# The mixer's latents, recurrence queries and first output turned by VectorE and a round trip through DRAM

## Chip, cores and metric

The kernel runs on one core of one Trainium2 chip. The metric is the device time of one execution in microseconds. The kernel before takes 1125.22 us, the median of three runs (1125.12 to 1125.36).

## What is computed

One layer of a streaming encoder on 256 tokens of width 2048, all float32. Cut to what matters here:

```python
h = rms_norm(x, attn_norm_w)
hq, hf, hi, hg, c_q, c_kv, k_r = split(h @ w_in)          # 1024 x4, 512, 512, 64
# first mixer: gated linear recurrence, 8 heads of 128
q = silu(hq); f = lb + (1 - lb) * sigmoid(hf); k = 1 - f
S_t = diag(f_t) S_{t-1} + k_t i_t^T;  o_t = S_t^T q_t
o_a = rms_norm(o, norm_w) * silu(hg)
# second mixer: latent attention, 8 heads
q = rms_norm(c_q, q_norm_w) @ w_uq;  kv = rms_norm(c_kv, kv_norm_w) @ w_ukv
o_b = softmax(masked(rope(norm(q)) @ rope(norm(k)).T)) @ v
x = x + concat([o_a, o_b]) @ w_out
x = x + (silu(n @ w_gate) * (n @ w_up)) @ w_down,  n = rms_norm(x, ffn_norm_w)
```

## The kernel before

Tokens lie on the partitions in two tiles of 128 (NT = 2). TensorE contracts over partitions, so every left operand has to be turned: features on the partitions, tokens in the row. Float32 precision comes from a split: a number is a rounded part "hi" and a rest "lo", and a product is hi x hi, lo x hi and hi x lo.

The weights come through a ring of four slots (`raw`, loaded by SyncE's queue, 512 KB each). ScalarE casts a slot to `w_hi` (line 757 up to the first eleventh of the feed-forward, 977 after), VectorE subtracts to `w_lo` (lines 1084, 1532). One slot is a granule: TensorE multiplies it in 12 matmuls (lines 1693, 1696). Granules 0 to 136 are the projections `lat` (3 blocks: the two latents and the rotary key), then hq0, uq0, hf0, ukv0, hi0, uq1, hg0, ukv1, hq1, uq2, ukv2, hf1, uq3, ukv3, hi1, hg1, then `w_out`. ScalarE may cast granule n only when TensorE is done with n - 4, and both conversions are written three granules ahead of TensorE (LEAD = 3).

Everything else in the mixers is a list of small steps, `schedule()`, each with a position, which is a granule's number. Each of the three engines goes through the same list in the same order: at position g, ScalarE and VectorE first convert granule g + 3 and then do their part of the steps of g, and TensorE does its part and then multiplies granule g. Within an engine all is in order, so a step that waits holds up the conversions behind it. END[block] is the number of the first granule behind a block: 17 and 25 for the blocks that complete the first and the second latent, 33 for hq0, 43 for hf0, 73 for hq1, 85 for hf1.

The steps that matter:

- `lat_a`, `lat_b` (18, 19 for the first latent, 26, 27 for the second): squares on ScalarE, reciprocal root, and the latent scaled by VectorE (line 1205). `lat_t` (22 and 30, two steps each): TensorE turns the latent in eight transposes through its identity matmul (line 1716) into PSUM banks, ScalarE writes the big half `mT_hi` (line 804), VectorE the small half `mT_lo` (line 1105). uq0 needs the first at granule 33, ukv0 the second at 43.
- `angles`, `sines` (29, 30): rotary angles, a long chain on VectorE, then ScalarE. `lb_a` to `lb_c`: the gates' lower bounds. `kr_b` (34): the rotary key.
- `hq` (33 and 73): the recurrence queries by ScalarE (line 897). `turn` (45 and 46 for the first half g = 0, 89 and 91 for the second): TensorE transposes queries (n = 0) and gates (n = 1) (line 1794), ScalarE copies them (line 905) or makes keys and logs (907, 910).
- `q_a`, `q_b`, `q_t` (35, 36, 39 for the first pair of heads): norm and rotation of attention queries into `stage` on VectorE, which TensorE transposes at position 39 (line 1751).
- `scan`, `lev_a`, `lev_b`, `pairs` (from 48 and 95): decays of the recurrence on VectorE and ScalarE, their products on TensorE (line 1805 for level 1).
- `o_a`, `o_b` (80, 81 for g = 0): norm of the recurrence's output, written to E by line 1403. `scores`, `softmax` (83, 84 for head 4), `hf_a` (84 for g = 1): forget gates, ScalarE 897, VectorE 1300 and 1301. `o_t` (95 for g = 0): eight transposes of the output and its split.

Small results of TensorE go through four side banks in turn; `side_uses` says which steps take one and who gives it back. The feed-forward already turns its hidden values as the change does: VectorE turns 32x32 blocks (line 1475), POOL writes them to DRAM and reads them back in four parts (lines 712, 718), with the same sizes.

Of the kernel before, what the change touches and what calls it, by code (L numbers as in the profile page):

```python
# [24 lines left out]
F32 = mybir.dt.float32  # L25
# [6 lines left out]
P = 128  # L32
D = 2048
SEQ = 256
NT = SEQ // P
# [179 lines left out]
def schedule():  # L215
# [32 lines left out]
    for g in range(2):  # L248
# [3 lines left out]
        s += [(e + 2 + 2 * g + n * (1 + g), ("turn", g, n, t)) for n in range(2) for t in range(NT)]  # L252
# [10 lines left out]
        s += [(p, ("o_a", g)), (p + 1, ("o_b", g))]  # L263
# [63 lines left out]
SPLIT = {step: n for n, step in enumerate(SPLITS)}  # L327

# [31 lines left out]
def hybrid_layer(nc, x, positions, attn_norm_w, w_in, hgrn_lb, hgrn_norm_w, mla_q_norm_w, w_uq, mla_kv_norm_w,  # L360
# [7 lines left out]
    with ExitStack() as ctx:  # L368
        def sb(name, shape, dt=F32, where=ctx):
            return where.enter_context(nc.sbuf_tensor(name, shape, dt))  # L370
# [75 lines left out]
        latents = (lat, hv)  # L446
        qTn = X[:, 0, :].rearrange("p (h t) -> p h t", h=HEADS)
# [9 lines left out]
        squares = nc.dram_tensor("squares", (P // Q, Q, P // Q, SEQ), F32, kind="Internal").ap()  # L457
        first_two = sb("first_two", [P, WIDE])
# [7 lines left out]
        corner, partly, both = gate[:, 0, :], gate[:, 1, :], hidden[:, 0, :]  # L466

# [45 lines left out]

        s_turned = sem("s_turned")
# [132 lines left out]
        def _(pool):  # L647
# [50 lines left out]

            pool.wait_ge(s_x[len(PIECES) - 1], 16)
            pool.dma_start(lb[:, :, :], hgrn_lb[:, 0:GW].partition_broadcast(P)).then_inc(s_lbin, 16)  # L700

            pool.wait_ge(s_lbused, 1)
            pool.wait_ge(s_side, USE[("join8", 0)] + 1)
            pool.dma_start(lb[:, :, :], hgrn_lb[:, GW:2 * GW].partition_broadcast(P)).then_inc(s_lbin, 16)

            pool.wait_ge(s_side, USE[("scores", HEADS - 1)] + 1)
# [41 lines left out]
        def _(act):  # L748
# [48 lines left out]

            def split_hi(parts):
# [8 lines left out]
            def step(s):  # L807
# [30 lines left out]
                elif kind == "lat_t":  # L838
                    i, j = a
                    ps, k, col = filled(s), 4 * i + 2 * j, (V_KVN if i else V_QN) + 2 * j  # L840
                    split_hi([(mT_hi[:, k + n, :], ps[:, n * SEQ:(n + 1) * SEQ], col + n) for n in range(2)])
# [46 lines left out]
                elif kind in ("hq", "hf_a", "hi", "hg"):  # L888
# [3 lines left out]
                    if kind == "hq" and not a[0]:  # L892
                        act.wait_ge(s_side, USE[("lat_t", 0, 1)] + 1)
                    if a[0] and kind == "hg":
                        act.wait_ge(s_given["dve"], GIVEN[USE[("o_a", 0, NT - 1)]])
# [3 lines left out]
                elif kind == "turn":  # L899
# [3 lines left out]
                    src = filled(s)[:, :].rearrange("p (h t) -> p h t", h=GH)  # L903
# [41 lines left out]
                elif kind == "o_t":  # L945
                    g, j = a
                    dst, k = (hT_hi, 12 + 2 * j) if g else (mT_hi, MT[HEADS + 2 * j])
                    split_hi([(dst[:, k:k + 2, :], filled(s)[:, :].rearrange("p (k t) -> p k t", k=2), V_HG)])
# [122 lines left out]
        def _(dve):  # L1071
# [26 lines left out]
            def split_lo(s, parts):  # L1098
# [8 lines left out]
                ins.then_inc(s_tlo, 1)  # L1107

                dve.wait_ge(s_tlo, SPLIT[s] + 1)
                dve.sem_inc(s_given["dve"], 1)  # L1110
# [61 lines left out]
            def step(s):  # L1172
# [33 lines left out]
                elif kind == "lat_t":  # L1206
                    i, j = a
                    ps, k, col = filled(s), 4 * i + 2 * j, (V_KVN if i else V_QN) + 2 * j
                    split_lo(s, [(mT_lo[:, k + n, :], ps[:, n * SEQ:(n + 1) * SEQ], mT_hi[:, k + n, :], col + n)
                                 for n in range(2)])  # L1210
# [98 lines left out]
                elif kind == "lev_a":  # L1309
# [3 lines left out]
                    if l == 1:  # L1313
                        if g:
                            dve.wait_ge(s_side, USE[("o_t", g - 1, 1)] + 1)
# [91 lines left out]
                elif kind == "o_t":  # L1407
                    g, j = a
                    hi, lo, k = (hT_hi, hT_lo, 12 + 2 * j) if g else (mT_hi, mT_lo, MT[HEADS + 2 * j])
# [623 lines left out]
```

## Time and profile before

| | us |
|---|---|
| median of three runs | 1125.22 |
| profiled execution | 1124.67 |
| span of the profiled execution, first to last instruction | 1122.9 |
| TensorE busy | 1113.2 |
| VectorE busy | 886.8 |
| ScalarE busy | 640.5 |
| granted TensorE clock | 1.0 |

Times of rows are counted from the span's start. The steps above end near 468 us; the feed-forward takes the rest. In a row of a timeline the first number is the start, the second how long the row lasts (several instructions when it ends in x2 or more), and a bracket at its end gives the engine's idle time before it and what ended that. PE is TensorE's matmuls, PEld its weight loads, DVE is VectorE, ACT ScalarE, POOL GpSimd.

### The profile page before, as it was taken

How to read it: one execution, taken by the hardware profiler on the slowest of the kernel's cores; microseconds unless marked ns; L12 is line 12 of the kernel's file. 1: busy time of each engine (PE TensorE's matmuls, PEld its weight loads, DVE VectorE, ACT ScalarE, POOL GpSimd, SP SyncE). 2: the span in 40 equal slices, each digit the busy share in tenths (PEclk: the TensorE clock that was granted, in tenths of full speed). 3: DMA queues.
4: the chain of work that ended last, by engine and by line, in shares of the span. 5: the costliest groups of instructions: out<-in, count | busy, mean ns of one | idle time of the engine just before them, and what ended most of it. 6: DMA issues, size and time to landing. Idle time of an engine off the chain costs nothing.

```text
span 1122.9 us, 15465 instructions
## 1 busy us (share of the span) xinstructions
PE 1113.2 (99%) x5265; PEld 937.8 (84%) x5265; DVE 886.8 (79%) x1198; ACT 640.5 (57%) x907; POOL 51.1 (5%) x134
## 2 busy tenths in 40 slices
PE   7999999999999999999999999999999999999998
PEld 7988888888888888888888888888888888888887
DVE  5578786587876667688888888888988879889777
ACT  7566776668664556454554554554554555555553
POOL 3000000000000000000000000000000010000000
PEclk9999999999999999999999999999999999999999
DMA  8666455545555455667777677777777686666655
GB/s 267 192 196 189 158 159 156 164 141 170 197 177 168 153 187 169 212 212 234 225 229 237 222 232 238 222 229 236 224 235 226 224 276 217 207 206 199 211 190 169
DMA packets 107239, 228.99 MB, mean 204 GB/s; under 512 B 8201, under 2 KB 19250, under 8 KB 106930
## 3 DMA queue, kind: packets, MB, share of 16 engines
q1 hardware_dynamic: 101346, 209.30, 58.9%
q0 software_dynamic: 5536, 18.88, 5.8%
q8 instruction: 29, 0.48, 0.2%
q14 instruction: 24, 0.20, 0.0%
q10 hardware_dynamic: 304, 0.14, 0.0%
HBM read 218.32 MB, written 9.96 MB: 203 GB/s over the span
## 4 chain that ended last, share of the span: by engine, by line
PE 97%; DVE 2%; DMA 1%; ACT 0%; issue 0%; SPq 0%; DVEq 0%; ACTq 0%
PE side L1919 25%; PE main L1693 22%; PE side L1921 12%; PE main L1696 11%; PE side L1891 4%; PE side L1892 4%; PE side L1893 4%; PE main L1893 3%; PE main L1891 3%; PE main L1892 3%; PE side L1817 1%; PE side L1716 1%; DMA raw<-in_w_in 1%; PE side L1764 0%; PE side L1765 0%; DVE w_lo L1084 0%
## 5 line engine op out<-in xcount | busy, mean ns | idle before, releaser
L977 ACT CAST w_hi<-raw 128x1024 fp32r<-128x1024 f32 (+1 forms) x245 | 241.6, 990 | 172.2 <-PE side L1919 104.9
L1532 DVE TENSOR_TENSOR w_lo<-raw,w_hi 128x1024 fp32r<-128x1024 f32 (+1 forms) x245 | 275.4, 1139 | 21.9 <-ACT w_hi L977 21.6
L1084 DVE TENSOR_TENSOR w_lo<-raw,w_hi 128x1024 fp32r<-128x1024 f32 (+3 forms) x156 | 178.5, 1154 | 107.9 <-ACT w_hi L757 105.6
L757 ACT CAST w_hi<-raw 128x1024 fp32r<-128x1024 f32 (+3 forms) x156 | 153.7, 993 | 142.5 <-PE main L1693 137.6
L1693 PE MATMUL main<-w_hi,hT_hi 128*128 128x512 f32 (+2 forms) x448 | 173.4, 388 | 1.7 <-DVE hT_lo L1105 1.4
L1696 PE MATMUL main<-w_hi,hT_lo 128*128 128x512 f32 (+2 forms) x448 | 169.1, 378 | 0.0
L1921 PE MATMUL side<-w_hi,hT_lo 128*128 128x512 f32 x400 | 155.6, 389 | 0.0
L1919 PE MATMUL side<-w_hi,hT_hi 128*128 128x512 f32 x400 | 155.6, 389 | 0.0
L1693 PE MATMUL main<-w_lo,hT_hi 128*128 128x512 f32 (+2 forms) x448 | 114.6, 377 | 0.0
L1919 PE MATMUL side<-w_lo,hT_hi 128*128 128x512 f32 x400 | 106.9, 389 | 0.0
L1693 PEld LDWEIGHTS main<-w_hi,hT_hi 128*128 128x128 f32 x448 | 84.7, 189 | 15.5 <-DVE hT_lo L1105 1.8
L1696 PEld LDWEIGHTS main<-w_hi,hT_lo 128*128 128x128 f32 x448 | 84.8, 189 | 13.0
L1693 PEld LDWEIGHTS main<-w_lo,hT_hi 128*128 128x128 f32 x448 | 82.9, 189 | 14.1
L1919 PEld LDWEIGHTS side<-w_hi,hT_hi 128*128 128x128 f32 x400 | 75.1, 188 | 15.6
L1919 PEld LDWEIGHTS side<-w_lo,hT_hi 128*128 128x128 f32 x400 | 75.1, 188 | 15.6
L1921 PEld LDWEIGHTS side<-w_hi,hT_lo 128*128 128x128 f32 x400 | 75.1, 188 | 15.5
L1921 PE MATMUL side<-w_hi,aT_lo 128*128 128x512 f32 x208 | 80.9, 389 | 0.0
L1919 PE MATMUL side<-w_hi,aT_hi 128*128 128x512 f32 x208 | 80.9, 389 | 0.0
L1532 DVE TENSOR_TENSOR w_lo<-last_two,w_hi 128x1024 fp32r<-128x1024 f32 x36 | 44.1, 1225 | 43.5 <-ACT w_hi L977 43.5
L977 ACT CAST w_hi<-last_two 128x1024 fp32r<-128x1024 f32 x36 | 37.9, 1052 | 59.9 <-PE side L1919 59.9
L977 ACT CAST w_hi<-first_two 128x1024 fp32r<-128x1024 f32 x36 | 38.0, 1056 | 58.4 <-PE side L1919 58.4
L1693 PE MATMUL main<-w_hi,mT_hi 128*128 128x512 f32 (+1 forms) x160 | 62.0, 387 | 0.0
(279 smaller groups left out, 1819.0 us busy)
## 6 DMA issues: line engine op xcount, KB each, us to landing
raw<-in_w_gate_up SPq DMA_DIRECT2D x176, 512.0 KB, 4.8
raw<-in_w_down SPq DMA_DIRECT2D x88, 512.0 KB, 4.5
raw<-in_w_in SPq DMA_DIRECT2D x64, 512.0 KB, 3.8
raw<-in_w_out SPq DMA_DIRECT2D x32, 512.0 KB, 3.7
raw<-in_w_in SPq DMA_DIRECT2D x15, 384.0 KB, 4.5
squares<-hiddenT POOLq DMA_DIRECT2D x11, 512.0 KB, 5.0
hiddenT<-squares POOLq DMA_DIRECT2D x44, 128.0 KB, 5.3
raw<-in_w_ukv SPq DMA_DIRECT2D x8, 512.0 KB, 3.9
```

The source lines that it names most:

```text
L757: copy(w_hi[:, slot, 0:n], raw[:, slot, 0:n]).then_inc(s_hi, 1)
L977: copy(w_hi[:, n % RING, 0:cols], src).then_inc(s_hi, 1)
L1084: tt(w_lo[:, slot, 0:n], raw[:, slot, 0:n], w_hi[:, slot, 0:n].bitcast(F32), ALU.subtract)\
L1532: tt(w_lo[:, n % RING, 0:cols], src, w_hi[:, n % RING, 0:cols].bitcast(F32), ALU.subtract)\
L1693: m = matmul(banks[t][:, 0:cols], hi[:, at[n], tok], rhs, start=(part == "hi" and k == k_first), stop=(part == "lo" and k == last))
L1696: matmul(banks[t][:, 0:cols], lo[:, at[n], tok], rhs, start=False, stop=False)
L1716: m = transpose(ps[:, at:at + P], where[:, t, (k + n) * P:(k + n + 1) * P], ident[:, :])
L1891: matmul(bank, hi, big, start=first, stop=False)
L1892: matmul(bank, lo, big, start=False, stop=False)
L1893: return matmul(bank, hi, small, start=False, stop=last)
L1919: m = matmul(bank, hi, rhs, start=False, stop=(part == "lo" and (t, half) in last))
L1921: matmul(bank, lo, rhs, start=False, stop=False)
```

## The change

Forty transposes leave TensorE: `lat_t` of both latents, `turn` with n = 0 of both halves, `o_t` of g = 0. In their place stands a new step, `swap`: VectorE turns the 128x1024 values in 32x32 blocks, POOL writes the result to DRAM (512 KB) and, once that has landed, reads it back in four parts of 128 KB that put the blocks where they belong. Positions: `swap` of the latents at 19 and 27, of the queries at 34 and 84, of the output at 81. The consumers wait for the landing: `lat_t` moves to 26, 27 (first latent) and 34, 35 (second), `turn` with n = 0 is at 45 and moves from 89 to 90 for g = 1, `o_t` stays at 95. The latents' and the output's small halves are made in four instructions of 128x128 a step. The turned data borrow buffers that are free at the time (`hbT`, `hkT`, E, `hgate`), which brings a few waits of order. POOL does the five round trips in the order first latent, second latent, queries 0, then the second load of the gate bounds, output 0, queries 1. All else is as before.

```diff
@@ schedule()
-        s += [(e + 1, ("lat_a", i)), (e + 2, ("lat_b", i))] + [(e + 5, ("lat_t", i, n)) for n in range(2)]
+        s += [(e + 1, ("lat_a", i)), (e + 2, ("lat_b", i)), (e + 2, ("swap", "lat", i))]
+        s += [(e + 9 + n, ("lat_t", i, n)) for n in range(2)]
...
-        s += [(e + 2 + 2 * g + n * (1 + g), ("turn", g, n, t)) for n in range(2) for t in range(NT)]
+        s += [(e - g if g else END[("hq", g)] + 1, ("swap", "hq", g))]
+        s += [(e + 2 + 3 * g + n, ("turn", g, n, t)) for n in range(2) for t in range(NT)]
...
-        s += [(p, ("o_a", g)), (p + 1, ("o_b", g))]
+        s += [(p, ("o_a", g)), (p + 1, ("o_b", g))] + [(p + 1, ("swap", "o", g))] * (g == 0)
@@ side_uses(step)
-    if kind in ("x", "x2", "lat_t", "o_t"):
+    if kind in ("x", "x2") or kind == "o_t" and step[1]:
         return [(step, "dve")]
-    if kind in ("vec", "turn", "probs_t", "join7", "join8"):
+    if kind in ("vec", "probs_t", "join7", "join8") or kind == "turn" and step[2]:
         return [(step, "act")]
@@ POOL
+            def swap(*key):
+
+                n, at = SWAP[key], swap_of[key]
+                pool.wait_ge(s_swap, n + 1)
+                pool.dma_start(swapped[n].rearrange("a c b x -> (a c) b x"), at).then_inc(s_parked, 16)
+                pool.wait_ge(s_parked, 16 * (n + 1))
+                for b in range(P // Q):
+                    pool.dma_start(at[Q * b:Q * (b + 1), :, :], swapped[n, :, :, b, :].rearrange("a c x -> c a x"))\
+                        .then_inc(s_landed, 16)
@@ ScalarE
+            def landed(*key):
+                act.wait_ge(s_landed, MOVED * (SWAP[key] + 1))
...
-                    ps, k, col = filled(s), 4 * i + 2 * j, (V_KVN if i else V_QN) + 2 * j
-                    split_hi([(mT_hi[:, k + n, :], ps[:, n * SEQ:(n + 1) * SEQ], col + n) for n in range(2)])
+                    k, col = 4 * i + 2 * j, (V_KVN if i else V_QN) + 2 * j
+                    landed("lat", i)
+                    split_hi([(by_quarter(mT_hi[:, k + n, :]), swapped_tile(("lat", i), 2 * j + n), col + n)
+                              for n in range(2)])
...
                     if n == 0:
-                        copy(hqT[:, :, t * P:(t + 1) * P], src).then_inc(s_given["act"], 1)
+                        landed("hq", g)
+                        src = swap_of[("hq", g)].rearrange("p a (t h r) -> p t h a r", t=NT, r=Q)[:, t, :, :, :]
+                        copy(hqT[:, :, t * P:(t + 1) * P].rearrange("p h (a r) -> p h a r", r=Q), src)
@@ VectorE
+            def swap(key, src):
+
+                nc.vector.transpose(swap_of[key].rearrange("p b (n r) -> p n b r", r=Q),
+                                    src.rearrange("p t (k b c) -> p (t k) b c", b=P // Q, c=Q)).then_inc(s_swap, 1)
...
-                    split_lo(s, [(mT_lo[:, k + n, :], ps[:, n * SEQ:(n + 1) * SEQ], mT_hi[:, k + n, :], col + n)
-                                 for n in range(2)])
+                    k, col = 4 * i + 2 * j, (V_KVN if i else V_QN) + 2 * j
+                    split_lo(s, [(by_quarter(mT_lo[:, k + n, :])[:, t, :, :], swapped_tile(("lat", i), 2 * j + n)[:, t, :, :],
+                                  by_quarter(mT_hi[:, k + n, :])[:, t, :, :], col + n) for n in range(2) for t in range(NT)])
@@ TensorE
-                elif kind == "lat_t":
-                    i, j = a
-                    pe.wait_ge(s_lat, NT * (i + 1))
-                    turn_x(s, 2 * j, latents[i])
...
-                elif kind == "turn":
+                elif kind == "turn" and a[1]:
...
-                elif kind == "o_t":
+                elif kind == "o_t" and a[0]:
```

## Rows read from the trace of the kernel before

**Rows 1.** The page, engines: busy us, share of the span, instructions.
```profile
PE 1113.2 (99%) x5265; PEld 937.8 (84%) x5265; DVE 886.8 (79%) x1198; ACT 640.5 (57%) x907; POOL 51.1 (5%) x134
```

**Rows 2.** The page, chain that ended last, by engine.
```profile
PE 97%; DVE 2%; DMA 1%; ACT 0%; issue 0%; SPq 0%; DVEq 0%; ACTq 0%
```

**Rows 3.** The page, groups: busy us, mean ns, idle before and its releaser.
```profile
L1084 DVE TENSOR_TENSOR w_lo<-raw,w_hi 128x1024 fp32r<-128x1024 f32 (+3 forms) x156 | 178.5, 1154 | 107.9 <-ACT w_hi L757 105.6
```

**Rows 4.** Transposes of queries (16) and first latent (8): ns min/median/max, first and last start.
```profile
L1794 PE MATMUL side<-ident,lat x16: 270/273/275, 116.5 to 265.5; 128*128 128x128 f32 x16
L1716 PE MATMUL side<-ident,lat x8: 270/272/273, 55.5 to 56.2; 128*128 128x128 f32 x8
```

**Rows 5.** Timeline of the weight loads around the first latent's transposes.
```profile
55.34 0.94 PEld L1716 LDWEIGHTS side<-ident,lat 128*128 128x128 f32 x8
...
56.24 0.19 PEld L1693 LDWEIGHTS main<-w_hi,hT_hi 128*128 128x128 f32 x1
```

**Rows 6.** Instructions on the feed-forward's turned values, waits, and time to landing.
```profile
L1475 DVE STREAM_TRANSPOSE hiddenT<-hidden x11: 1233/1235/1240, 471.3 to 895.1; 128x1024 f32<-128x1024 f32 x11
...
DMA squares<-hiddenT: 53.4, 11
...
DMA to landing us min/median/max: 3.4/5.3/7.2
```

**Rows 7.** Timeline of POOL, first round trip of the feed-forward.
```profile
472.86 0.57 POOL L712 DMA_DIRECT2D squares<-hiddenT  x1 [173.26 <-DVE hiddenT L1475]
478.57 2.20 POOL L718 DMA_DIRECT2D hiddenT<-squares  x4 [5.14 <-DMA squares<-hiddenT]
```

**Rows 8.** Timelines of ScalarE and VectorE: both halves now, four 128x128 elsewhere.
```profile
56.69 1.56 ACT L804 ACTIVATE mT_hi<-side,vec_cols 128x256 fp32r<-128x256 f32 x4
...
57.96 0.87 DVE L1105 SCALAR_TENSOR_TENSOR mT_lo<-side,vec_cols,mT_hi 128x256 fp32r<-128x256 f32 x2
...
123.34 1.13 DVE L1263 SCALAR_TENSOR_TENSOR stage<-main,stat,kw_row 128x128 f32<-128x128 f32 x4
```

**Rows 9.** Timeline of VectorE, 50 to 100 us.
```profile
52.94 0.89 DVE L1205 TENSOR_SCALAR lat<-lat,stat 128x512 f32<-128x512 f32 x2
...
73.87 1.23 DVE L1084 TENSOR_TENSOR w_lo<-raw,w_hi 128x1024 fp32r<-128x1024 f32 x1 [1.34 <-ACT w_hi L757]
...
90.62 1.23 DVE L1084 TENSOR_TENSOR w_lo<-raw,w_hi 128x1024 fp32r<-128x1024 f32 x1 [2.78 <-ACT w_hi L757]
...
98.65 0.28 DVE L1140 TENSOR_TENSOR stage_r<-rot 128x128 f32<-128x128 f32 x1
```

**Rows 10.** Timeline of ScalarE, 60 to 90 us.
```profile
64.64 1.05 ACT L757 CAST w_hi<-raw 128x1024 fp32r<-128x1024 f32 x1 [1.69 <-PE main L1693]
65.59 0.63 ACT L779 ACTIVATE hlf<-hv 128x512 f32<-128x512 f32 x1
...
84.59 1.06 ACT L757 CAST w_hi<-raw 128x1024 fp32r<-128x1024 f32 x1 [1.35 <-PE main L1693]
```

**Rows 11.** Timeline of TensorE: the query stage's first transposes.
```profile
99.45 0.60 PE L1751 MATMUL side<-ident,stage 128*128 128x128 f32 x4
```

**Rows 12.** Timeline of ScalarE, last wait for TensorE before the recurrence's first half.
```profile
111.27 1.05 ACT L757 CAST w_hi<-raw 128x1024 fp32r<-128x1024 f32 x1 [1.67 <-PE main L1693]
```

**Rows 13.** Line 1805, level 1 products: what TensorE waited for (us, times).
```profile
DVE E L1339: 0.5, 1
```

**Rows 14.** Timeline of VectorE, 245 to 262 us.
```profile
245.72 2.16 DVE L1403 SCALAR_TENSOR_TENSOR E<-side,stat,hgate 128x128 f32<-128x128 f32 x8
...
257.43 1.23 DVE L1300 TENSOR_TENSOR hlf<-hlf,E 128x1024 f32<-128x1024 f32 x1 [1.83 <-ACT hlf L897]
...
259.84 2.35 DVE L1084 TENSOR_TENSOR w_lo<-raw,w_hi 128x1024 fp32r<-128x1024 f32 x2
```

**Rows 15.** Timeline of TensorE, granule whose w_lo starts at 259.84.
```profile
261.20 0.47 PE L1693 MATMUL main<-w_hi,mT_hi 128*128 128x512 f32 x1
```

**Rows 16.** The page: busy tenths of the DMA engines in 40 slices of 28 us.
```profile
DMA  8666455545555455667777677777777686666655
```

More of the change, by code:

```diff
@@ L327 @@
 SPLIT = {step: n for n, step in enumerate(SPLITS)}
+SWAPS = [step[1:] for _, step in SCHEDULE if step[0] == "swap"]
+SWAP = {key: n for n, key in enumerate(SWAPS)}
 RMS = [step for _, step in SCHEDULE if step[0] in ("r1a", "lat_a", "q_a", "k_a", "o_a", "r2a")]
@@ L446, in hybrid_layer @@
         latents = (lat, hv)
+        swap_of = {("lat", 0): hbT[:, :, :], ("lat", 1): hkT[:, :, :], ("o", 0): hgate.rearrange("p t (a c) -> p (t a) c", a=2)}
+        for g in range(2):
+            swap_of[("hq", g)] = E[:, g, :].rearrange("p (a c) -> p a c", a=P // Q)
         qTn = X[:, 0, :].rearrange("p (h t) -> p h t", h=HEADS)
@@ L512, in hybrid_layer @@
         s_join = sem("s_join")
+        s_swap = sem("s_swap")
+        s_parked = sem("s_parked")
+        s_landed = sem("s_landed")
         s_turned = sem("s_turned")
@@ L891, in step @@
                                "hg": (hgate, ACT.Silu)}[kind]
-                    if kind == "hq" and not a[0]:
-                        act.wait_ge(s_side, USE[("lat_t", 0, 1)] + 1)
+                    if kind == "hq":
+                        act.wait_ge(s_swap, SWAP[("hq", 0) if a[0] else ("lat", 0)] + 1)
                     if a[0] and kind == "hg":
-                        act.wait_ge(s_given["dve"], GIVEN[USE[("o_a", 0, NT - 1)]])
+                        act.wait_ge(s_tlo, SPLIT[("o_t", 0, 1)] + 1)
                     for t in range(NT):
@@ L946, in step @@
                     g, j = a
-                    dst, k = (hT_hi, 12 + 2 * j) if g else (mT_hi, MT[HEADS + 2 * j])
-                    split_hi([(dst[:, k:k + 2, :], filled(s)[:, :].rearrange("p (k t) -> p k t", k=2), V_HG)])
+                    if not g:
+                        landed("o", g)
+                        split_hi([(by_quarter(mT_hi[:, MT[HEADS + 2 * j + n], :]), swapped_tile(("o", g), 2 * j + n), V_HG)
+                                  for n in range(2)])
+                        return
+                    k = 12 + 2 * j
+                    split_hi([(hT_hi[:, k:k + 2, :], filled(s)[:, :].rearrange("p (k t) -> p k t", k=2), V_HG)])
                 elif kind == "sq2":
@@ L1408, in step @@
                     g, j = a
-                    hi, lo, k = (hT_hi, hT_lo, 12 + 2 * j) if g else (mT_hi, mT_lo, MT[HEADS + 2 * j])
-                    split_lo(s, [(lo[:, k:k + 2, :], filled(s)[:, :].rearrange("p (k t) -> p k t", k=2),
-                                  hi[:, k:k + 2, :], V_HG)])
+                    if not g:
+                        at = [MT[HEADS + 2 * j + n] for n in range(2)]
+                        split_lo(s, [(by_quarter(mT_lo[:, k, :])[:, t, :, :], swapped_tile(("o", g), 2 * j + n)[:, t, :, :],
+                                      by_quarter(mT_hi[:, k, :])[:, t, :, :], V_HG)
+                                     for n, k in enumerate(at) for t in range(NT)])
+                        return
+                    k = 12 + 2 * j
+                    split_lo(s, [(hT_lo[:, k:k + 2, :], filled(s)[:, :].rearrange("p (k t) -> p k t", k=2),
+                                  hT_hi[:, k:k + 2, :], V_HG)])
                 elif kind in ("out1", "out2"):
```

44 lines of the change are left out of this document (33 added, 11 removed).

## The prediction

> **What bounds the kernel now.** The page comes first: TensorE is busy for 99% of the span, VectorE for 79% [rows 1], and the chain that ended last is TensorE for 97% [rows 2]. So time taken off TensorE comes off the kernel, as long as nothing else makes TensorE wait. Next, what TensorE depends on. Each step of the first 137 ("granules", 12 matmuls each) needs its weights split by ScalarE (w_hi) and then VectorE (w_lo). The groups by line show that VectorE spends 107.9 us waiting ahead of w_lo, nearly always for w_hi [rows 3]: on average there is room. But both queues run in order, with the mixer's small steps between the conversions, so the average says little; the timelines of ScalarE and VectorE have to be followed where the edited steps stand. There the reader should look at the bracket at the end of a row: it is the idle time ahead of the instruction. A stretch without brackets has no room, and whatever is put into it arrives later at the far end. "ACT waits for PE main" is the good case: the engine has caught up and is paced by TensorE.
>
> **What is removed.** 40 transposes on TensorE: 8 for each of the two latents, 16 for the recurrence queries [rows 4], 8 for the first output, all of one form. Eight of them hold the weight-load queue from 55.34 to 56.24, 0.90 us, before the next granule's load [rows 5]. Five groups of eight: 5 x 0.90 = 4.5 us. Of these 1.8 us lie before the position of the first query transposes at 99.45. With the transposes go their PSUM banks and a 0.2 us wait after each split on VectorE, which matter little.
>
> **What is added, instruction by instruction.** (a) Five VectorE turns of 128x1024: this very instruction stands in the later stage with 1.235 us [rows 6], so 6.2 us of VectorE. (b) Five round trips on POOL's queue: one write, a wait, four reads. The later stage makes the same trip 11 times. In the first the write is issued at 472.86 and the first read at 478.57, 5.7 us, and the four read issues take 2.20 us, so the last begins 1.65 us after the first [rows 7]. Over all 11, POOL idles 53.4 / 11 = 4.85 us behind the write's own 0.56: 5.4. An issue lands after 5.3 us, at least 3.4 and at most 7.2 [rows 6]. Ahead of it 0.3 us pass from the turn's end to the write, an estimate from the first turn (start 471.3, 1.24 long). From the end of a turn to the data: 0.3 + 5.4 + 1.65 + 5.3 = 12.7 us, between 10.7 (with 3.4) and 14.9 (with 5.7 and 7.2). I take 12.7, since size, queue and neighbours are alike. (c) The small halves of the latents and the first output become four instructions of 128x128 where there were two of 128x256 (or one of 128x512). Four scalar_tensor_tensor of that size take 1.13 us in another step [rows 8], the two old ones 0.87 plus the 0.2 us that goes: no change in length, but the latents' steps move to other positions, and that counts. ScalarE's big halves cost 0.39 us an instruction as before [rows 8]; the query copies read SBUF instead of PSUM, a tenth of a us or so. On POOL nothing else suffers: the second load of the gate bounds, which now stands behind three trips, waits for the last product of the first half anyway.
>
> **The first trip is late.** The first latent is scaled until 52.94 + 0.89 = 53.83 [rows 9]. Turn 1.24, trip 12.7: landed at 67.8, between 65.8 and 70.0. ScalarE comes to the step that reads it (position 26) straight after the w_hi cast of 64.64; that cast is paced by TensorE, which is 0.9 us earlier by then, so ScalarE is there at 64.8 [rows 10]. It stops for 3.0 us, and behind it in its queue stand the squares of the second latent, the next conversions and all else.
>
> **How far that carries.** From here I follow the chain in the old timelines. From the squares at 65.59 [rows 10] to the end of the query stage, 98.65 + 0.28 = 98.93 [rows 9], there are 33.3 us: squares, w_hi, w_lo, the scaling of the second latent, two w_lo, the angle arithmetic, sine and table loads, three casts, the queries' activation with two table loads, then VectorE's w_lo, rotary key, two w_lo and query stage. In this path two idle times disappear once it runs late: 1.34 before the w_lo of 73.87 [rows 9] and 1.35 before the cast of 84.59 [rows 10]. 33.3 - 2.7 = 30.6. Added into it: the latent's big half on ScalarE 0.8, its small half 1.1, the second latent's turn 1.3 (with its wait), the two steps of the second latent, now behind the cast at position 34 and 35, 2.3, and the turn of the recurrence queries 1.2: 6.7 us. From 90.62 on VectorE has no bracket up to the stage's end [rows 9], so the last 3.5 of these are paid in full. The stage is ready at 67.8 + 30.6 + 6.7 = 105.1. TensorE transposes it at 99.45 now, 0.5 us after it is ready [rows 11], and would want it at 99.45 - 1.8 = 97.65. With 0.2 us from VectorE to TensorE's matmul it waits until 105.3, less some 0.3 for ends and starts of instructions that overlap: 7.3 us, in one piece or in several before it (w_lo of the granules between is late by 0.5 to 2 us by the same chain, inside this sum). With the trip's bounds: 5.3 to 9.5.
>
> **The recurrence's first half.** ScalarE is paced by TensorE at 111.27 for the last time, then table loads, activations, copies and scan run without a gap until the level products, for which TensorE already waits a little, 0.5 us by the summary of that line [rows 12, 13]. Between the two TensorE loses one group of eight transposes. It arrives 0.9 us earlier and waits 0.9 us longer: that group's saving is lost.
>
> **Around 250 us.** VectorE runs without a bracket from the first output (245.72) to the scores, whose maximum ScalarE needs before it can go to the forget gate; VectorE then waits for that gate, multiplies it, and goes to w_lo at 259.84, done 1.2 later, 0.15 us ahead of TensorE's matmul at 261.20 [rows 14, 15]. The change puts the first output's turn right after 245.72 and the second queries' turn right before 259.84: 1.24 + 1.24 - 0.15 = 2.3 us of wait. The second queries' own trip: turned at 262.3, landed at 275.0; ScalarE, delayed too, gets there at about 274, and the group's transposes are gone from TensorE, so I count nothing; if the cover fails it costs up to 3 us (rival 3). The first output has from 249 to 286: free, 0.2 us for the longer split ahead of the second scan.
>
> **Sum.** The profiled execution took 1124.67 us (span 1122.9), the median is 1125.2. Against the median: 1125.2 - 4.5 + 7.3 + 0.9 + 2.3 + 0.2 = 1131.4; against the profiled execution, 0.5 under the median, 1130.9.
>
> **Rival 1, faster.** The lead of the conversions takes in all of it: w_lo waits for w_hi for 107.9 us in all [rows 3], and the two brackets of 1.34 and 2.78 on VectorE alone [rows 9] are over 4 us, most of what the late trip and a turn add. Then only the recurrence's 0.9 is lost: 1125.2 - 4.5 + 0.9 = 1121.6. It needs the query stage to be ready within about 0.5 us of now. Against it: those gaps stand ahead of the pieces that wait, and from 90.62 there is none, yet 3.5 us are added. Chance 0.12.
>
> **Rival 2, slower by less.** The first trip is in time, at or before 64.8. The chain then starts when ScalarE arrives: 64.8 + 30.6 + 6.7 = 102.1, a wait of 4.3 instead of 7.3 (102.1 - 0.1 - 97.65 again), and 1128.4. For it: the DMA engines are busy for four to seven tenths before 460 us and for six to eight after it [rows 16], so the 5.4 and 5.3 may shrink. Against it: the trip would have to take 9.7 us, and the lower bound is 10.7. Chance 0.17, with 1127 to 1129 as its own range.
> The Trainium skill, in DMA: Bandwidth & Descriptors, section on the anatomy of one DMA on the gpsimd path, gives 2.0 us plus the bytes over 436 GB/s for one transfer. By it the write would be 3.2 us, a read 2.3, the trip 7.5, an estimate from that page, and rival 2 would hold. The rows show 5.7 and 5.3 for the same two transfers in this kernel, beside weight loads that share the DMA engines, so the trace does not agree and the chance stays small.
>
> **Rival 3, slower by more.** The second queries' trip is late as well, and ScalarE's stop there delays the log of the gates, which holds the PSUM banks of the next key transposes: 2 to 3 us more, about 1134. It decides if the trip takes over 14 us. Chance 0.13.
>
> **How the numbers follow.** Forecast 0.55, rival 1 0.12, rival 2 0.17, rival 3 0.13, the rest between forecast and no change. The forecast's own range by the trip's bounds is 1129.2 to 1133.5; the range to hold 8 in 10 leaves out rival 1 and reaches 1126 to 1135. A difference of 0.2% (2.25 us) is about what can be told from none. Rival 2's lower edge falls within it: same 0.07; faster 0.12; slower 0.81.
>
> **What would show it.** In the new profile: ScalarE idle some 3 us before the first latent's big half, ended by a DMA; TensorE idle near 98 to 105 for 5 us or more in sum, ended by VectorE's w_lo or stage; TensorE idle for 1 us before the level products near 139, and for 2 us at the granule after 254; about 6.2 us more of VectorE in the turns. Wrong if the first trip takes under 10 us, if the small halves cost clearly less than 0.28 each, or if TensorE's idle time up to 110 us hardly grows.

## The result and the profile after

The changed kernel takes 1133.13 us, the median of five runs (1133.0 to 1137.55), against 1125.31 for the kernel before on the same chip: a ratio of 1.0077, 95% interval 1.0059 to 1.0096, slower by 7.8 us. The forecast of 1131.4 was 1.7 too low; its sign and its mechanism hold, with every term that adds time somewhat too small.

The profiled execution has a span of 1131.4 us. First the page: engines, the chain by engine, and a group of its fifth part, for rows 1 to 3.

```profile
PE 1110.7 (98%) x5225; PEld 933.0 (82%) x5225; DVE 894.4 (79%) x1217; ACT 640.7 (57%) x909; POOL 64.6 (6%) x159
...
PE 87%; DVE 6%; ACT 3%; issue 2%; DMA 2%; SPq 0%; POOL 0%; DVEq 0%; ACTq 0%
...
L1133 DVE TENSOR_TENSOR w_lo<-raw,w_hi 128x1024 fp32r<-128x1024 f32 (+3 forms) x156 | 178.4, 1154 | 106.8 <-ACT w_hi L792 104.7
```

TensorE has 40 instructions less, yet its share of the chain that ended last falls from 97% [rows 2] to 87%: the chain now runs through VectorE, ScalarE and a transfer. The idle time ahead of w_lo is still 106.8 us, against 107.9 [rows 3]; that sum hides everything that happened. What TensorE's matmuls waited for in the first 470 us says more (us in total, times, longest):

```profile
PE main L1767 <- DVE w_lo L1133: 4.8, 5, 1.6
...
PE side L1821 <- DVE stage_r L1194: 2.5, 1, 2.5
...
PE side L1871 <- DVE E L1407: 1.1, 1, 1.1
...
PE side L1844 <- DVE probs L1357: 0.8, 1, 0.8
```

w_lo and stage_r are new here. The level products (L1871) wait 1.1 us, which isn't to be set against the 0.5 of [rows 13]: that is the idle time of the weight-load queue. Like for like, the first weight load of the level products waits 1.56 instead of 0.55, and the first matmul 1.14 instead of nothing:

```profile
139.65 2.05 PE L1805 MATMUL side<-E 128*128 128x128 f32 x16
```

That is the kernel before; the row at 146.60 below is the same step. Where the waits stand, from TensorE's timeline of the changed kernel:

```profile
79.58 0.47 PE L1767 MATMUL main<-w_hi,hT_hi 128*128 128x512 f32 x1 [1.62 <-DVE w_lo L1133]
...
106.23 0.66 PE L1821 MATMUL side<-ident,stage 128*128 128x128 f32 x4 [2.53 <-DVE stage_r L1194]
...
146.60 2.05 PE L1871 MATMUL side<-E 128*128 128x128 f32 x16 [1.14 <-DVE E L1407]
...
270.77 0.47 PE L1767 MATMUL main<-w_hi,mT_hi 128*128 128x512 f32 x1 [1.45 <-DVE w_lo L1133]
```

Subtracting the times at which TensorE ended each granule in the two traces gives the whole account. Delays are in us, minus is gained:

| granules | what | change |
|---|---|---|
| 2 to 4 | first loads, ahead of every edited step | +0.69 |
| 23, 31, 46, 90, 96 | five groups of transposes gone | -4.49 |
| 32 to 39 | w_lo late (1.90, 1.19, 0.53, 1.35, 0.22) | +5.19 |
| 40 | query stage late | +2.75 |
| 53 | first level products | +1.01 |
| 87, 89, 90 | probabilities, w_lo, w_lo (1.00, 1.55, 0.46) | +3.01 |
| 100 | level products of the second half | +0.39 |

The sum is 8.55, the spans differ by 8.5; after granule 100 nothing changes. The 0.69 is not the change's: the same stretch differs by -0.3 to +2.5 between the profiles of all kernels below, so traces are compared net of it. Net of it the change costs 7.9, and 7.8 by the medians.

The chain behind the waits up to granule 40 begins with the first round trip. VectorE's turn, POOL's queue, and the two places where ScalarE stops, from their timelines:

```profile
54.55 1.25 DVE L1163 STREAM_TRANSPOSE hbT<-lat 128x1024 f32<-128x1024 f32 x1
...
56.11 0.56 POOL L723 DMA_DIRECT2D swapped<-hbT  x1 [36.97 <-DVE hbT L1163]
60.11 2.21 POOL L726 DMA_DIRECT2D hbT<-swapped  x4 [3.44 <-DMA swapped<-hbT]
...
61.19 1.05 ACT L792 CAST w_hi<-raw 128x1024 fp32r<-128x1024 f32 x1 [1.96 <-DMA raw<-in_w_in]
...
69.37 0.91 ACT L842 ACTIVATE mT_hi<-hbT,vec_cols 128x256 fp32r<-128x256 f32 x2 [3.87 <-DMA hbT<-swapped]
```

The turn ends at 55.80, the data are there at 69.3: 13.5 us, and ScalarE stands still for 3.87. It also stops for 1.96 for weights at 61.19, which it never does between 50 and 100 us in the kernel before. What follows on VectorE, from its timeline:

```profile
70.32 1.14 DVE L1154 SCALAR_TENSOR_TENSOR mT_lo<-hbT,vec_cols,mT_hi 128x128 fp32r<-128x128 f32 x4 [3.10 <-ACT mT_hi L842]
...
94.63 1.23 DVE L1133 TENSOR_TENSOR w_lo<-raw,w_hi 128x1024 fp32r<-128x1024 f32 x1 [1.61 <-ACT w_hi L792]
95.77 1.13 DVE L1154 SCALAR_TENSOR_TENSOR mT_lo<-hkT,vec_cols,mT_hi 128x128 fp32r<-128x128 f32 x4
...
98.20 1.25 DVE L1163 STREAM_TRANSPOSE E<-lat 128x1024 f32<-128x1024 f32 x1
...
105.89 0.29 DVE L1194 TENSOR_TENSOR stage_r<-rot 128x128 f32<-128x128 f32 x1
```

From 94.63 to the stage at 106.18 there is no bracket, and a turn (1.25) and both small halves of the second latent (1.13 each) stand in that stretch: 3.5 us of new work on the path. From start to next start they take 1.17, 1.05 and 1.02, and w_lo at its head is 4.0 later than in the kernel before, the end 7.25 later: it stood at 98.93 [rows 9].

### The profile page after: what moved, and what is told of

The parts are those of the page before. It is cut to its first block, busy times and chain, and to the rows that moved or that the text cites. A ratio compares the mean times of both kernels' runs of the same rounds, so it can differ in the third digit from the quotient of the medians.

```text
span 1131.4 us, 15412 instructions
## 1 busy us (share of the span) xinstructions
PE 1110.7 (98%) x5225; PEld 933.0 (82%) x5225; DVE 894.4 (79%) x1217; ACT 640.7 (57%) x909; POOL 64.6 (6%) x159
## 4 chain that ended last, share of the span: by engine, by line
PE 87%; DVE 6%; ACT 3%; issue 2%; DMA 2%; SPq 0%; POOL 0%; DVEq 0%; ACTq 0%
PE side L1985 24%; PE main L1767 17%; PE side L1987 12%; PE main L1770 8%; PE side L1957 4%; PE side L1958 4%; PE side L1959 4%; PE main L1958 3%; PE main L1959 3%; PE main L1957 3%; DVE w_lo L1133 2%; PE side L1883 1%; ACT w_hi L792 1%; DMA hbT<-swapped 1%; DMA raw<-in_w_in 1%
## 5 line engine op out<-in xcount | busy, mean ns | idle before, releaser
L1133 DVE TENSOR_TENSOR w_lo<-raw,w_hi 128x1024 fp32r<-128x1024 f32 (+3 forms) x156 | 178.4, 1154 | 106.8 <-ACT w_hi L792 104.7
L1985 PE MATMUL side<-w_hi,aT_hi 128*128 128x512 f32 x208 | 80.9, 389 | 0.0
L1987 PE MATMUL side<-w_hi,aT_lo 128*128 128x512 f32 x208 | 80.9, 389 | 0.0
```

The costliest lines, as they stand in the source:

```text
L1133: tt(w_lo[:, slot, 0:n], raw[:, slot, 0:n], w_hi[:, slot, 0:n].bitcast(F32), ALU.subtract)\
L1985: m = matmul(bank, hi, rhs, start=False, stop=(part == "lo" and (t, half) in last))
L1987: matmul(bank, lo, rhs, start=False, stop=False)
```

## Experiments

Differences below are medians against the kernel before on the same chip (1124.9 to 1125.1). "Net" is the delay of TensorE from the trace, as in the table above, without granules 2 to 4. Where an interval holds 1 (the first queries alone, the first output alone, four groups) the medians alone tell no difference, and the reading rests on the traces; with the first queries moved it just reaches 1. The diffs are shortened. In them, SWAPPED lists the groups that go the new way while all others are as in the kernel before; SWAP_AT gives a turn another position, LAT_T_AT a latent's two steps of halves.

### Is it the trip? Consumers that don't wait for it

```diff
             def landed(*key):
-                act.wait_ge(s_landed, MOVED * (SWAP[key] + 1))
+                act.wait_ge(s_swap, SWAP[key] + 1)
@@ POOL
-            swap("lat", 0)
-            swap("lat", 1)
-            swap("hq", 0)
...
-            swap("o", 0)
-            swap("hq", 1)
```

> The change without its 25 transfers: the consumers read the turned buffers as soon as VectorE has written them, so the blocks stand in the wrong places; all instructions of the engines stay. Theory of the late trip: with the change ScalarE idled 3.9 us before the first latent's big half; here it goes on at once, the query stage is ready 3.9 us earlier, and the rest of the waits stays: 1133.1 - 3.9 = 1129.2 us. Rival, traffic: the five round trips slow the weight loads (landing 4.4 us instead of 3.8 for the projections), and that is the whole loss; without them 4.5 us are won on the kernel before, 1121 to 1123. Rival, VectorE's work alone: nothing changes, 1133.

Measured 1130.64 (1129.62 to 1131.28), ratio 1.0048 [1.0031, 1.0065], +5.6. ScalarE's big half now follows the cast at once:

```profile
66.23 1.05 ACT L797 CAST w_hi<-raw 128x1024 fp32r<-128x1024 f32 x1 [1.63 <-PE main L1803]
67.19 0.91 ACT L847 ACTIVATE mT_hi<-hbT,vec_cols 128x256 fp32r<-128x256 f32 x2
```

The net delay is 3.85 instead of 7.88, the 4.0 that was expected; the medians give only 2.2 between the two kernels. The traces explain most of that gap. This profile is 2.5 late at the first loads, and 1.6 of it is TensorE's granted clock, which stands at its lower level (1.2 GHz) for 3.4 us from 18.05:

```profile
18.00:20.00 2.00, 2.00 (x9) 0.51 0.84 253
```

(TensorE's busy time in that stretch, with its instructions in brackets, then the granted clock, the DMA share and GB/s.) The mean granted clock of an execution tells of such a stretch: it is 0.998 in three of this kernel's four, and 1.0 in the fourth, which took 1129.62, 4.6 over the kernel before and 3.5 under the changed kernel's median execution, whose clock was full too. So the transfers cost 3.5 to 4 us of the 7.8, on one execution and one trace, and some 4 stay without them: 2.75 at the query stage, 0.99 at granule 36 and what the later places cost. The rival of traffic alone (1121 to 1123) is out.

### The first latent's halves later

```diff
-        s += [(e + 9 + n, ("lat_t", i, n)) for n in range(2)]
+        at = {0: (28, 29)}.get(i, (e + 9, e + 10))
+        s += [(at[n], ("lat_t", i, n)) for n in range(2)]
```

> The change with the first latent's halves made at positions 28 and 29 instead of 26 and 27, trips and all else kept. Theory of the late trip: the squares, conversions and scaling of the second latent no longer stand behind the landing. By the old timelines the angles then end near 80.9, the cast that follows is 0.9 us behind TensorE, and the query stage makes TensorE wait 4.0 us instead of 7.95: about 1129.2. Rival, traffic: the same transfers at the same times, so 1133.

Measured 1131.04 (1130.5 to 1132.51), ratio 1.0052 [1.0035, 1.0069], +6.0: 2.1 us better than the change where 4 were expected. A miss, and its timelines of ScalarE (first row) and VectorE say why:

```profile
69.25 1.05 ACT L799 CAST w_hi<-raw 128x1024 fp32r<-128x1024 f32 x1 [1.08 <-DMA raw<-in_w_in]
...
70.34 1.23 DVE L1159 TENSOR_TENSOR w_lo<-raw,w_hi 128x1024 fp32r<-128x1024 f32 x1 [2.73 <-ACT w_hi L799]
...
72.97 1.25 DVE L1189 STREAM_TRANSPOSE hkT<-hv 128x1024 f32<-128x1024 f32 x1
...
75.25 1.13 DVE L1180 SCALAR_TENSOR_TENSOR mT_lo<-hbT,vec_cols,mT_hi 128x128 fp32r<-128x128 f32 x4
...
77.43 1.13 DVE L1180 SCALAR_TENSOR_TENSOR mT_lo<-hbT,vec_cols,mT_hi 128x128 fp32r<-128x128 f32 x4
...
83.07 0.23 DVE L1250 TENSOR_SCALAR sincos<-sincos 128x128 f32<-128x128 f32 x1
```

ScalarE no longer stops for the landing, but both small halves and the second latent's turn (3.5 us) now stand right ahead of the angles, which end at 83.3 instead of the 80.9 on which the expectation rested; 85.3 in the changed kernel. And the w_lo ahead of them starts at 70.34, 1.5 later than the 68.80 of the kernel before, behind a cast that waits 1.08 for weights; between 50 and 100 us ScalarE waits 3.4 for weights. The query stage then ends at 104.19, 2.0 before the changed kernel's 106.18, as the medians have it. The profile's net delay is only 0.4 smaller, because in this execution, and not in the others (clock 1.0), the granted clock is at its lower level from 103.8 to 107.2; the same matmul of granule 40 takes 0.78 here and 0.47 in the changed kernel:

```profile
104.00:107.50 3.50, 3.25 (x11) 0.54 0.86 224
...
105.44 0.78 PE L1805 MATMUL main<-w_hi,hT_hi 128*128 128x512 f32 x1
```

### Parts alone: both latents; first output and second queries

Each is the kernel before with the named groups turned the new way, at the positions of the change.

```diff
@@ both latents
+SWAPPED = [("lat", 0), ("lat", 1)]
@@ first output and second queries
+SWAPPED = [("hq", 1), ("o", 0)]
```

> Only the two latents go through VectorE and DRAM; queries and output stay on TensorE. Theory of the ordered chains: the query stage is late by the chain without the queries' turn (1.25 us less), a wait of 6.7 instead of 7.95, against 1.8 us of transposes saved: before + 4.9 = 1130.2. Rival, traffic: two of five trips, + 3.1 = 1128.4.

Measured 1130.12 (1129.36 to 1130.86), ratio 1.0046 [1.0029, 1.0063], +5.05.

> Only the first output and the second half's queries go through VectorE and DRAM. Theory of the ordered chains: the two turns make TensorE wait 1.0 at the probabilities' transposes and 1.55 at the second granule after, 0.46 one later and 0.4 before the level products, against 1.8 us saved: before + 1.6 = 1126.9. Rival, traffic: two of five trips, + 3.1 = 1128.4.

Measured 1126.47 (1125.77 to 1128.04), ratio 1.0011 [1.0002, 1.0021], +1.4. Both are close to their expectations, and their sum of 6.45 leaves 1.4 for the first queries: the two stretches, up to 110 us and around 250 us, act little on each other.

### The turns alone

The kernel before with five more instructions on VectorE, in line 1186.

```diff
@@ schedule(), kernel before
+        s += [(e + 2, ("swap", "lat", i))]
...
+        s += [(e - g if g else END[("hq", g)] + 1, ("swap", "hq", g))]
...
+        s += [(p + 1, ("swap", "o", g))] * (g == 0)
```

> The kernel before, with the five VectorE turns of the change added at their five positions (19, 27, 34, 81, 84); nobody reads what they write, there is no round trip, and TensorE keeps all 40 transposes. Theory (VectorE's order of work sets the price): the latents' turns fit into VectorE's idle times of 1.53 and 1.34 us ahead of the w_lo at 68.80 and 73.87, the turn of queries 0 has only 0.5 us of slack before the query stage and costs 0.75, the two turns around 250 us cost 2.3. Sum 3.0, 1128.1. Rival (the transfers and what waits for them carry the price, VectorE's leads take in the turns): within 0.5 of the kernel before, 1125.1 to 1125.6.

Measured 1127.85 (1127.58 to 1129.76), ratio 1.0027 [1.0018, 1.0036], +3.0, as the theory had it. In the trace the latents' turns cost nothing, the first queries' turn 0.70 at granule 40, the two late ones 1.08 at 87 and 1.57 at 89. Two rows of VectorE, the turn behind an idle time and the one without:

```profile
90.64 1.23 DVE L1156 TENSOR_TENSOR w_lo<-raw,w_hi 128x1024 fp32r<-128x1024 f32 x1 [2.79 <-ACT w_hi L794]
...
93.17 1.25 DVE L1186 STREAM_TRANSPOSE E<-lat 128x1024 f32<-128x1024 f32 x1
```

The idle time of 2.79 is still there, 2.5 us ahead of the turn that would fit into it. This is the position's price, not the instruction's.

### The first queries alone

```diff
+SWAPPED = [("hq", 0)]
```

> Queries 0 alone go the new way, everything else as in the kernel before. Theory: the turn costs 0.75 ahead of the query stage, and the 0.90 us of transposes taken off TensorE are lost as a wait before the level products, so 1125.8, with the wait for the stage at about 0.7 us and the one for the level products up by 0.9. Rival (the transfer beside the weight loads delays the conversions as well): 1126.5 to 1127.5, with waits of w_lo at the granules 32 to 36 as in the changed kernel.

Measured 1125.63 (1125.26 to 1126.53), ratio 1.0006 [0.9997, 1.0015], +0.77. TensorE's timeline:

```profile
100.12 0.66 PE L1863 MATMUL side<-ident,stage 128*128 128x128 f32 x4 [0.51 <-DVE stage_r L1220]
...
140.45 2.05 PE L1917 MATMUL side<-E 128*128 128x128 f32 x16 [1.11 <-DVE E L1440]
```

By granules: +0.70 at 40, -0.89 at 46, +0.96 at 53. What the transposes saved comes back in full as a wait for the level products. With the parts before: 5.05 + 1.40 + 0.77 = 7.2 of the 7.8. A rest of 0.6 is within the intervals of the medians; the traces leave 0.7 (5.0, 1.4 and 0.8 of 7.9), of which 0.26 stands at granule 90.

### The first output's turn in an idle time

```diff
+SWAPPED = [("o", 0)]
...
-... [(p + 1, ("swap", "o", g))] * (g == 0)
+... [(84, ("swap", "o", g))] * (g == 0)
```

> The first output alone goes the new way, and its turn stands at position 84 between the softmax of head 4 and the forget gate, where VectorE idles 1.83 us for ScalarE's sigmoid. Theory: the turn of 1.24 us costs nothing there, the trip has 25 us, TensorE loses 0.90 us of transposes: 1124.2. Rival (VectorE is late for w_lo whatever the place of the turn, as with the position 81 of the change): 1125.2 to 1125.5.

Measured 1124.44 (1123.74 to 1126.13), ratio 0.9997 [0.9988, 1.0006], -0.4. The turn is free:

```profile
255.64 1.24 DVE L1189 STREAM_TRANSPOSE hgate<-E 128x1024 f32<-128x1024 f32 x1
257.55 1.23 DVE L1399 TENSOR_TENSOR hlf<-hlf,E 128x1024 f32<-128x1024 f32 x1 [0.67 <-ACT hlf L956]
```

The bracket of 1.83 [rows 14] has become 0.67 and the gate is multiplied at the same time as before. TensorE gains 0.92 at granule 96 and loses 0.40 at 100, which the expectation had left out: the small halves, eight instructions in 2.18 us at 290.03, stand straight ahead of the second scan.

### Second latent and first output

```diff
+SWAPPED = [("lat", 1), ("o", 0)]
+SWAP_AT = {("o", 0): 84}
+LAT_T_AT = {1: (37, 38)}
```

> Second latent and first output go the new way, the latent's halves at 37 and 38 (behind the query stage's arithmetic instead of ahead of the angles), the output's turn at 84. Theory: the latent's turn fits the 1.34 us gap at 73.87, 1.95 us of small halves leave VectorE's and 0.8 us ScalarE's work ahead of the query stage, so the stage follows TensorE's earlier arrival, and both groups' 0.90 us are won: 1123.3. Rival (the small halves at 37 and 38, 2.3 us, stand ahead of the gates' bounds and the level products and come back there): the output's 0.9 alone, 1124.2, or worse, 1125.

Measured 1123.51 (1123.19 to 1125.44), ratio 0.9986 [0.9977, 0.9995], -1.35. By granules -0.88 at 31 and -0.87 at 96, +0.39 at 100: the latent's group is won whole, the missing 0.4 is again the second scan.

### The first queries' turn in an idle time, their copies earlier

```diff
+SWAPPED = [("hq", 0)]
+SWAP_AT = {("hq", 0): 33}
...
-        s += [(e + 2 + 2 * g + n * (1 + g), ("turn", g, n, t)) ...]
+        s += [(e + 2 + 2 * g + n * (1 + g) - 3 * (n == 0 and g == 0), ("turn", g, n, t)) ...]
```

> Queries 0 alone go the new way, with the turn at position 33 (in VectorE's idle time of 2.78 us ahead of the w_lo at 90.62, before the rotary key) and the ScalarE copies at 42, ahead of its last wait for TensorE (1.67 us at 111.27), instead of 34 and 45. Theory: the turn costs nothing there, 1.1 us of copies leave the stretch without a gap that ends in the level products, and the 0.9 us of transposes are won at last: 1124.0. Rival (what TensorE saves ahead of the level products is lost in any case, as their chain hangs on the gates): 1124.9, as the kernel before.

Measured 1124.1 (1123.86 to 1125.91), ratio 0.9991 [0.9982, 1.0], -1.0. VectorE, around the turn:

```profile
87.99 1.25 DVE L1189 STREAM_TRANSPOSE E<-lat 128x1024 f32<-128x1024 f32 x1 [0.41 <-ACT lat L956]
90.35 1.23 DVE L1159 TENSOR_TENSOR w_lo<-raw,w_hi 128x1024 fp32r<-128x1024 f32 x1 [1.11 <-ACT w_hi L799]
```

The idle time of 2.78 [rows 9] now holds the turn. One position earlier for it and three for the copies turn +0.77 into -1.0; neither granule 40 nor 53 loses anything. The copies, at 42, come after granule 40, so the 0.70 there is the turn's alone; at 53 the two moves were not tried apart.

### Three groups, each where it fits

```diff
+SWAPPED = [("hq", 0), ("lat", 1), ("o", 0)]
+SWAP_AT = {("hq", 0): 33, ("o", 0): 84}
+LAT_T_AT = {1: (37, 38)}
...
-        s += [(p, ("o_t", g, 0)), (p, ("o_t", g, 1))]
+        s += [((93 + n) if g == 0 else p, ("o_t", g, n)) for n in range(2)]
```

(with the copies of the queries at 42 as above)

> Second latent (halves at 37, 38), queries 0 (33, copies at 42) and first output (turn at 84, halves at 93 and 94 instead of 95) go the new way. Theory: each group's 0.9 us is won, and the halves at 93 and 94 fill VectorE's idle times of 0.67 and 0.99 us at 285.16 and 287.38, so that the wait of 0.4 us at the second half's level products goes: 1122.2. Rival (three trips close together and 2.3 us of halves more at 37 and 38 take back the queries' share): 1123.1 to 1123.5.

Measured 1122.01 (1121.64 to 1124.66), ratio 0.9974 [0.9965, 0.9983], -3.1: faster than the kernel before, and 11 us faster than the change. By granules -0.91 at 31, -0.89 at 46, -0.96 at 96 and nothing at 100. VectorE, at the output's halves and the second scan:

```profile
283.01 1.14 DVE L1180 SCALAR_TENSOR_TENSOR mT_lo<-hgate,vec_cols,mT_hi 128x128 fp32r<-128x128 f32 x4 [0.53 <-ACT mT_hi L849]
...
285.20 1.13 DVE L1180 SCALAR_TENSOR_TENSOR mT_lo<-hgate,vec_cols,mT_hi 128x128 fp32r<-128x128 f32 x4
...
288.82 2.43 DVE L1406 TENSOR_TENSOR_SCAN hbT<-keep,logT 128x256 f32<-128x256 f32 x4
```

The scan starts at 288.82, 3.0 earlier than the kernel before (291.81), and TensorE is 2.9 earlier there.

### The first latent as well, with and without its transfers

```diff
+SWAPPED = [("hq", 0), ("lat", 0), ("lat", 1), ("o", 0)]
+LAT_T_AT = {0: (28, 29), 1: (37, 38)}
```

> As the one with three groups, and the first latent too, its halves at 28 and 29. Theory: the first trip still lands near 68 to 69, VectorE then works without a gap from about 70.3 with 30.3 us of work to the query stage (33.9 in the kernel with the late halves, less 2.3 for the second latent's halves and 1.2 for the queries' turn), ready at 100.7 where TensorE comes at 97.6: a wait of 3.1 us for 0.9 more saved: 1124.4. Rival (the late start is taken in, as the other trips are): 1121.3.

Measured 1125.1 (1124.38 to 1126.54), ratio 1.0002 [0.9993, 1.0011]: one more group of transposes less, and 3.1 us more. The place differs from the expectation. TensorE waits 2.4 at granules 34 to 36 (0.50, 0.54, 1.35), and nothing at the query stage. That is 1.5 of the 3.1, net of the transposes saved; another 1.1 in this trace is a wait near 529 us, in the feed-forward, which the next kernel has too (1.2) and the one with three groups hasn't. Its cause stays open; the run with the first queries at 33 has a like one (1.0) near 923. ScalarE's timeline:

```profile
61.44 1.05 ACT L799 CAST w_hi<-raw 128x1024 fp32r<-128x1024 f32 x1 [2.33 <-DMA raw<-in_w_in]
...
70.90 1.05 ACT L799 CAST w_hi<-raw 128x1024 fp32r<-128x1024 f32 x1 [1.04 <-DMA raw<-in_w_in]
...
82.58 0.31 ACT L872 ACTIVATE sincos<-sincos 128x128 f32<-128x128 f32 x1 [5.24 <-DVE sincos L1250]
```

Weights come late at 61 and 71, the landing is never waited for, and the angles are late. To part the two causes, the same kernel without transfers:

```diff
-                act.wait_ge(s_landed, MOVED * (SWAP[key] + 1))
+                act.wait_ge(s_swap, SWAP[key] + 1)
@@ POOL
-                if key in (("lat", 0), ("lat", 1), ("hq", 0)):
-                    swap(*key)
...
-                if key in (("o", 0), ("hq", 1)):
-                    swap(*key)
```

> The kernel with four groups, without its 20 transfers: the consumers read what VectorE has just turned, with the blocks in the wrong places, so the values are wrong and only the work and its times count. Every turn, copy and half stays where it is. In the kernel with four groups ScalarE waits 4.3 us in all for weights between 50 and 100 us, which the kernel before doesn't. Theory (the first trip's transfers share the DMA engines with the weight loads and start VectorE's stretch some 0.9 us late): 1124.2, with 1.5 us or less of waits for weights, and the angles done at 81.5 instead of 82.5. Rival (VectorE's 2.3 us of halves ahead of the angles are the whole price): 1125.0.

Measured 1122.72 (1122.14 to 1124.59), ratio 0.9979 [0.997, 0.9988], -2.3. The same two places of ScalarE:

```profile
59.66 1.05 ACT L797 CAST w_hi<-raw 128x1024 fp32r<-128x1024 f32 x1 [1.08 <-DMA raw<-in_w_in]
...
80.91 0.31 ACT L870 ACTIVATE sincos<-sincos 128x128 f32<-128x128 f32 x1 [4.09 <-DVE sincos L1248]
```

The transfers alone cost 2.4 us in the medians (2.25 if each is taken against the kernel before on its own chip), more than the 0.9 of the theory. Waits for weights between 50 and 100 us fall from 4.3 to 1.1 us and the sine starts 1.7 earlier, of which 0.5 is the first loads. The rival is not empty: without transfers TensorE still waits 1.27 at granule 36, the price of 2.3 us of halves ahead of the angles, so even then a fourth group gains nothing over three. Of the 2.4 the traces place 1.2 at granules 34 to 36; the rest is not placed. The next three rows are the stretch from 60 to 70 us, ScalarE busy, granted clock, and in the last two columns the share of the DMA engines (it can come out slightly over 1) and GB/s. The kernel before:

```profile
60.00:70.00 10.00, 6.44 (x14) 1.00 0.75 242
```

The changed kernel:

```profile
60.00:70.00 10.00, 3.79 (x5) 1.00 1.05 344
```

Four groups without transfers:

```profile
60.00:70.00 10.00, 6.86 (x15) 1.00 0.84 262
```

In these 10 us the first trip's transfers and the weights together have the DMA engines fully busy, which neither of the others shows. It isn't the whole of it: the changed kernel without transfers has a share of 0.94 at 313 GB/s there, and its ScalarE still waits 1.5 us for weights between 50 and 100, against 2.3 with them and none in the kernel before. What makes weights late without a trip was not tried.

## Why the prediction was right, step by step

| term of the sum | predicted | trace |
|---|---|---|
| five groups of transposes | -4.5 | -4.49 |
| late first trip, carried to the query stage | +7.3 | +7.94 |
| first half of the recurrence | +0.9 | +1.01 |
| around 250 us | +2.3 | +3.01 |
| second scan | +0.2 | +0.39 |

In sum -4.5 + 12.4 = 7.9 in the trace, where -4.5 + 10.7 = 6.2 was forecast: every term that adds time was too small, none by more than some 0.7.

The trip: near in sum, by two misses that cancel in part, which is luck. POOL's write to its first read took 4.0 us, not 5.4; but the reads landed later. The view of DMA issues between 50 and 112 us (KB each, median us to landing):

```profile
swapped<-hbT POOLq DMA_DIRECT2D x1, 512.0 KB, 3.7
hbT<-swapped POOLq DMA_DIRECT2D x4, 128.0 KB, 6.6
swapped<-hkT POOLq DMA_DIRECT2D x1, 512.0 KB, 3.2
hkT<-swapped POOLq DMA_DIRECT2D x4, 128.0 KB, 4.0
```

The first trip's reads took 6.6 in the median where 5.3 was assumed [rows 6], and the last was there 7.5 after its issue at 61.8, above the 7.2 taken as bound. In sum 13.5 from turn to data, for 12.7, and ScalarE stopped for 3.87, for 3.0; without the transfers 3.5 to 4 came back. The other four trips of the changed kernel took 9.7, 11.0, 11.2 and 10.1, so one figure for all of them was too coarse: 12.7 lies between the first and the rest. The rule weighed in the prediction (the Trainium skill, DMA: Bandwidth & Descriptors, section on the anatomy of one DMA on the gpsimd path) gives 3.2 us for the write, an estimate from that page: the trace agrees in the second trip's 3.2, and the first one's 3.7 lies 0.5 above. Its 2.3 for a read, an estimate too, is far below the medians of 4.0 to 6.6 in these rows. So the trip of 7.5, and with it rival 2, did not come.

The chain: 37.3 us of squares, conversions, angles, sine and new work were added up; the trace has 36.0 from the squares at 70.19 to the stage's end, 36.8 with the big half ahead. Both brackets that were struck out are gone. The 0.5 less comes of the overlap of neighbours: a turn takes 1.17 to the next start and four small halves 1.02 to 1.05, where 1.2 to 1.3 and 1.1 to 1.15 were counted. So the last 3.5 us are paid nearly in full, with 3.25. The turn's share of it is shown by the run with the turns alone (0.70 for the query turn, 0.75 by the prediction's slack of 0.5). By its own terms the forecast's range comes to 1129.4 to 1133.6, not 1129.2 to 1133.5.

The level products: the forecast read the 0.5 of [rows 13] as a wait of TensorE. It is the weight-load queue's, and the matmuls waited for nothing. The term hangs on the chain that has no gap and not on this 0.5, and it holds: 0.9 forecast, 1.01 in the trace.

Where the sum was wrong by a size: the term around 250 us. 1.24 + 1.24 less 0.15 was counted; granules 87 and 89 took 2.55, so two turns with next to no slack, and another 0.46 followed at granule 90, where the kernel with the turns alone has no such loss (2.51 in all there) and the one with the first output and second queries alone 0.2. What makes it was not tried.

Rival 1 (the lead takes in everything) fails at the place where the prediction put its doubt: the gaps exist, but ahead of the pieces that wait. Moved to stand right ahead of gaps, three groups do bring all of their 2.7 us (3.1 by the medians): the leads are there, for another order of the steps. Rival 3 did not happen, as POOL's and ScalarE's timelines show:

```profile
269.81 0.56 POOL L723 DMA_DIRECT2D swapped<-E  x1 [7.23 <-DVE E L1163]
273.43 2.19 POOL L726 DMA_DIRECT2D E<-swapped  x4 [3.06 <-DMA swapped<-E]
...
281.27 1.15 ACT L946 COPY hqT<-E 128x512 f32<-128x512 f32 x2
```

ScalarE comes to the copies at 281.27 without a wait for the landing.

What the prediction didn't see is the second way in which a trip costs: not by its latency but by the weights that arrive late beside it. In the changed kernel ScalarE's waits for weights, at 61.19 and 62.61, are taken in before its stop for the landing: at 64.45 it waits for TensorE again, 0.79. So the sum came out nearly right without that term.

## What to carry to other kernels

Work that is moved from a full engine to one with 20% idle time costs nothing only in front of an idle time: the same turn cost 0.70 at position 34 and nothing at 33, and around 250 us nothing where it stood behind the softmax. So read the brackets of the engine that takes the work, and place each step ahead of one, the consumers' halves too. A round trip through DRAM took 9.7 to 13.5 us from turn to data in the changed kernel and up to 15.4 in the one with three groups; it needs that distance and a stretch in which the weight loads have room. The group that has neither (the first latent, 3.1 us worse by the medians) is left where it was. And look at the granted clock of a profiled execution before its time is set against another: one short stretch at the lower level was worth 1.4 to 1.6 us here, half of some effects above.

## What the runs showed of the hardware

- With the first trip beside the weights the DMA engines were fully busy at 344 GB/s from 60 to 70 us, and a read of 128 KB took 6.6 us there, against 4.0 in the second trip some twenty microseconds later.
- The write of 512 KB over POOL's queue landed in 3.2 to 3.7 us in the changed kernel's mixers, in 3.2 to 5.3 in the kernels with three and four groups; the same write in the feed-forward had POOL wait 4.85 behind it [rows 6].
- ScalarE's big half costs 0.45 us read from SBUF in runs of 32 (four in 1.8) against 0.39 out of PSUM [rows 8]; VectorE's four small halves of 128x128 cost 1.13, as elsewhere [rows 8].
- In three of the profiled executions (no transfers; first latent later; second latent and first output) TensorE's granted clock stood at 0.5, its lower level of 1.2 GHz, for 3.4 us. In the second of them weight loads then took 0.33 us instead of 0.19, and the clock fell at 103.8, while TensorE had been idle since 101.7; the changed kernel has an idle time of the same length (2.53) at its query stage and full clock behind it. What decides between the two, the runs don't show.
